# Two layer norms around a gated ConvFFN on one core: statistics from running sums, and an up-projection of rows that are not yet normalised

## What is computed

```python
x1 = layer_norm(ALPHA * x + mix @ w_out, ln1_w, ln1_b)
u, fconv_new = causal_dwconv(x1 @ w_up + b_up, fconv_prev, ffn_conv_w, ffn_conv_b)   # width 3
ff = (jax.nn.gelu(u[..., :D_FF]) * u[..., D_FF:]) @ w_down + b_down                  # D_FF = 2688
y = layer_norm(ALPHA * x1 + ff, ln2_w, ln2_b)
```

## Time and profile before

| | us |
|---|---|
| median of 3 runs | 1031.28 |
| lowest, highest | 1025.5, 1032.95 |
| profiled execution, whole | 1037.76 |
| profiled execution, span first to last instruction | 1036.1 |
| PE busy in it | 917.0 |
| DVE busy | 517.5 |
| ACT busy | 374.2 |
| POOL busy | 99.3 |

### The profile page before, as it was taken

One profiled execution on the slowest core, in us unless ns is written; L12 is line 12 of the kernel. 1 busy time (PEld: TensorE's weight loads), 2 busy tenths in 40 slices (PEclk: granted clock), 3 DMA queues, 4 the chain that ended last, 5 costly groups with the idle time before them and its releaser, 6 DMA issues.

```text
span 1036.1 us, 19860 instructions
## 1 busy us (share of the span) xinstructions
PE 917.0 (89%) x7903; PEld 821.8 (79%) x7903; DVE 517.5 (50%) x1116; ACT 374.2 (36%) x742; POOL 99.3 (10%) x164
## 2 busy tenths in 40 slices
PE   5999988998898667888869959999999999999993
PEld 5888877787776553655559839999999999999992
DVE  4522345522335566566752265766776677332325
ACT  4322344644421010345651155434433443222115
POOL 1012213343341002000000000000000000000000
PEclk9989999899896555569989969999999999999997
DMA  8247777676462001400022202222222222222212
GB/s 292 70 145 256 229 264 235 207 223 180 127 233 89 6 1 42 175 1 1 2 87 82 82 1 75 89 82 85 100 82 82 95 90 72 89 90 76 86 33 87
DMA packets 53152, 112.46 MB, mean 109 GB/s; under 512 B 6954, under 2 KB 30283, under 8 KB 52611
## 3 DMA queue, kind: packets, MB, share of 16 engines
q1 hardware_dynamic: 45648, 91.68, 25.9%
q0 software_dynamic: 6528, 17.83, 5.4%
q10 hardware_dynamic: 882, 1.67, 0.5%
HBM read 105.54 MB, written 12.40 MB: 114 GB/s over the span
## 4 chain that ended last, share of the span: by engine, by line
PE 80%; DVE 9%; ACT 4%; issue 3%; DMA 3%; ACTq 0%; POOLq 0%; POOL 0%; SPq 0%; DVEq 0%
PE q L1669 30%; PE q L1667 27%; PE q L2114 3%; DMA arena<-in_pool 2%; PE q L2142 2%; PE q L2132 2%; PE q L1731 1%; PE q L2175 1%; PE q L2176 1%; PE q L2002 1%; PE q L2056 1%; PE q L1719 1%; PE q L1785 1%; ACT whi L956 1%; PE q L1965 1%
## 5 line engine op out<-in xcount | busy, mean ns | idle before, releaser
L469 DVE TENSOR_TENSOR wring_r<-wring,whi_r 128x1024 fp32r<-128x1024 f32 (+1 forms) x101 | 120.5, 1194 | 341.8 <-ACT whi_r L466 341.7
L466 ACT ACTIVATE whi_r<-wring 128x1024 fp32r<-128x1024 f32 (+1 forms) x101 | 104.2, 1033 | 327.8 <-PE q L1669 316.9
L1669 PE MATMUL q<-xt_r,whi_r 128*128 128x288 f32 x552 | 166.9, 302 | 0.0
L1667 PE MATMUL q<-xt_r,whi_r 128*128 128x256 f32 x552 | 157.5, 285 | 0.0
L1667 PE MATMUL q<-arena_r,whi_r 128*128 128x256 f32 x440 | 137.6, 313 | 19.6 <-DVE xt_r L469 11.5
L1669 PE MATMUL q<-arena_r,whi_r 128*128 128x288 f32 x440 | 133.7, 304 | 0.0
L1669 PE MATMUL q<-arena_r,wring_r 128*128 128x288 f32 x440 | 133.0, 302 | 0.0
L1667 PE MATMUL q<-arena_r,wring_r 128*128 128x256 f32 x440 | 125.9, 286 | 0.0
L1667 PE MATMUL q<-mixt_r,whi_r 128*128 128x256 f32 x400 | 113.2, 283 | 10.5 <-DVE xt_r L469 10.5
L1669 PE MATMUL q<-mixt_r,whi_r 128*128 128x288 f32 x400 | 119.4, 298 | 0.0
L1667 PEld LDWEIGHTS q<-arena_r,whi_r 128*128 128x128 f32 x440 | 86.2, 196 | 27.4 <-issue 19.7
(11 more groups left out here) (406 smaller groups left out, 1584.1 us busy)
## 6 DMA issues: line engine op xcount, KB each, us to landing
wring<-in_w_up SPq DMA_DIRECT2D x42, 512.0 KB, 3.2
wring<-in_w_in SPq DMA_DIRECT2D x27, 512.0 KB, 5.1
arena<-in_pool SPq DMA_DIRECT2D x64, 192.0 KB, 3.1
arena<-in_pool POOLq DMA_DIRECT2D x64, 192.0 KB, 3.9
wring<-in_w_down SPq DMA_DIRECT2D x24, 448.0 KB, 3.1
arena<-in_pool SPq DMA_DIRECT2D x64, 64.0 KB, 2.1
arena<-in_pool POOLq DMA_DIRECT2D x64, 64.0 KB, 2.4
wring<-in_w_out SPq DMA_DIRECT2D x8, 512.0 KB, 7.3
```

The lines of the kernel that those rows point to most:

```text
L466: return eng.activation(out, src, ACT.Copy)
L469: return eng.tensor_tensor(out, src, hi.bitcast(F32), ALU.subtract)
L1667: pe.matmul(out[:, 0, 0:HALF], w, x[:, 0:HALF], start=(kk == 0 and n == 0), stop=(end and n == 2))
L1669: mm = pe.matmul(out[:, 1, 0:HALF + NS], w, x[:, HALF:NT], start=(kk == 0 and n == 0), stop=(end and n == 2))
```

## The change

- **Running sums.** In the out and down stages DVE keeps `total`, the sum of the rows so far, and `squares`, the sum of the squares that ACT makes. All rows are shifted by the mean of tile 0's rows times 8 (`shift`): PE makes it after four k steps of tile 1 (`first_mean`). The averages after each tile are gone.
- **Raw rows into the up stage.** The up tiles multiply the shifted, unnormalised rows times `ln1_w`, split as they come (`raw_high` on ACT, `raw_low` on DVE). Two more columns, `ln1_w` and `ln1_b` themselves, go along, so each tile's second matmul is 290 wide and its last two columns hold what the mean is to be multiplied by and the product with the bias.
- **Statistics per token in five columns.** `token_means` multiplies blocks of 128 tokens as the stationary operand with one column of `avg`, which gives mean and mean square of a token in a partition: five columns in all. DVE forms variance and reciprocal on those, spreads them over a diagonal, and PE's `spread` brings the factor of each token into every partition.
- **Mean and deviation at eviction.** In the up stage DVE's `scaled_rows` reads PSUM, subtracts and multiplies by `rstd`; ACT then writes `u` from SBUF, and takes over the convolution's first tap (`f_one`). The history copies go to POOL.
- **Down stage.** DVE rebuilds `ALPHA * x1 + b_down` from the raw rows (`residual`), then adds PSUM directly (`added`).

The core of the diff:

```diff
+        shift, total, squares, sq_m = (smem[:, NT * n:NT * n + NT] for n in range(4))
+        mean, rstd = dsc[:, 0:NT], dsc[:, NT:2 * NT]
...
+            for n in range(UP):
+                pool.wait_ge(f_u, n + 1)
+                pool.tensor_copy(fc[:, n, 0:2], uf[:, n % 4, 512:514])
+                pool.tensor_copy(fc[:, n, 2:18].rearrange("p (b t) -> p b t", b=NB),
+                                 by_sequence(uf, n, 6)[:, :, 4:6]).then_inc(f_last, 1)
...
+                if n == 0:
+                    root(0)
                 split_hi(act, I_UP + n + 2)
+                if n == 0:
+                    act.wait_ge(ln_pe, pe_stat(0, "mean"))
+                    act.activation(mean[:, 0:T].rearrange("p (c t) -> p c t", c=2), q4[2][:, :, 0:HALF], ACT.Copy)
+                    act.activation(mean[:, T:NT], q4[2][:, 1, HALF:HALF + NS], ACT.Copy)
+                    act.wait_ge(ln_pe, pe_stat(0, "spread"))
+                    act.activation(rstd[:, 0:T], bank[6], ACT.Copy)
+                    act.activation(rstd[:, T:NT], bank[7][:, 0:NS], ACT.Copy).then_inc(ln_act, 1)
                 if n >= 4:
                     act.wait_ge(f_conv, n - 3)
-                u = uf[:, n % 4, :]
+                    act.wait_ge(f_last, n - 3)
+                    act.wait_ge(f_done, (n - 4) // 2 + 1)
+                u, b, t = uf[:, n % 4, :], rowsum[:, n % 2:n % 2 + 1], scaled[n % 2]
                 us = by_sequence(uf, n, 6)
                 act.activation(us[:, :, 0:2], hf[:, n, :].rearrange("p (b t) -> p b t", b=NB), ACT.Copy)
-                act.activation(u[:, 2:514].rearrange("p (c t) -> p c t", c=2), q4[n % 2][:, :, 0:HALF],
-                               ACT.Identity, bias=vec("b_up", n))
-                act.activation(us[:, :, 2:6], q4[n % 2][:, 1, HALF:HALF + NS].rearrange("p (b t) -> p b t", b=NB),
-                               ACT.Identity, bias=vec("b_up", n)).then_inc(f_u, 1)
+                act.wait_ge(rw_u, n + 1)
+                act.activation(u[:, 2:514], t[:, 0:T], ACT.Identity, bias=b, scale=-1.0)
+                act.activation(us[:, :, 2:6], t[:, T:NT].rearrange("p (b t) -> p b t", b=NB), ACT.Identity,
+                               bias=b, scale=-1.0).then_inc(f_u, 1)
+                act.wait_ge(f_u, n + 1)
+                act.activation(tf[:, n % 4, 0:560], u[:, 0:560], ACT.Identity, bias=vec("fconv_b", n),
+                               scale=vec("fconv_w", n)).then_inc(f_one, 1)
...
+                    link(dve.tensor_tensor(t, raw_lo[:, m, 0:NT].bitcast(F32), raw_hi[:, m, 0:NT].bitcast(F32), ALU.add))
+                    link(dve.tensor_tensor(t, t, rstd, ALU.mult))
+                    link(dve.scalar_tensor_tensor(out=t, in0=mean, scalar=vec("ln1_w", m), in1=t, op0=ALU.mult,
+                                                  op1=ALU.subtract))
+                    link(dve.tensor_scalar(t, t, -ALPHA, var[:, m:m + 1], ALU.mult, ALU.add))
+                    if m >= 1:
+                        link(dve.tensor_tensor(t, t, shift, ALU.subtract))
...
+            def sums(base, m):
+                dve.wait_ge(ln_d, shifted_rows(base // KD, m))
+                link(dve.tensor_tensor(total, total, xt[:, m, :], ALU.add))
+            def sums_of_squares(base, m):
+                dve.wait_ge(ln_q, base + m + 1)
+                dve.tensor_tensor(squares, squares, sq_m, ALU.add).then_inc(ln_a, 1)
+                dve.wait_ge(ln_a, (KD - 1) * (base // KD) + m)
+            def raw_low(m):
+                dve.wait_ge(rw_hi, m + 1 if m == 0 else m + 2)
+                dve.scalar_tensor_tensor(out=raw_lo[:, m, 0:NT], in0=xt[:, m, :], scalar=vec("ln1_w", m),
+                                         in1=raw_hi[:, m, 0:NT].bitcast(F32), op0=ALU.mult,
+                                         op1=ALU.subtract).then_inc(rw_lo, 1)
...
+            def variance(n):
+                dve.wait_ge(ln_pe, pe_stat(n, "tokens"))
+                link(dve.tensor_copy(var[:, 8:13], bank[6][:, 0:5]))
+                link(dve.tensor_tensor(var[:, 8:13], var[:, 8:13], var[:, 8:13], ALU.mult))
+                dve.tensor_tensor(tok5[:, :], bank[7][:, 0:5], var[:, 8:13], ALU.subtract).then_inc(ln_dve, 1)
+            def inverse(n):
+                dve.wait_ge(ln_act, act_stat(n, "root"))
+                link(dve.reciprocal(tok5[:, :], tok5[:, :]))
+                dg = scaled[0]
+                dve.tensor_tensor(by_block(dg[:, 0:T]), ident.unsqueeze(1).broadcast_to([128, 4, 128]),
+                                  bc(tok5[:, 0:4], 128), ALU.mult)
+                dve.tensor_tensor(dg[:, T:NT], ident[:, 128 - NS:128], tok5[:, 4:5].broadcast_to([128, NS]),
+                                  ALU.mult).then_inc(ln_dve, 1)
...
+            def scaled_rows(n):
+                p, t = q4[n % 2], scaled[n % 2]
+                dve.wait_ge(w_used, I_UP + n + 1)
...
+                c1 = p[:, 1, HALF + NS:HALF + NS + 1]
+                dve.tensor_scalar(rowsum[:, n % 2:n % 2 + 1], p[:, 1, HALF + NS + 1:HALF + NS + 2], vec("b_up", n), None,
+                                  ALU.add)
+                dve.scalar_tensor_tensor(out=t[:, 0:T].rearrange("p (c t) -> p c t", c=2),
+                                         in0=mean[:, 0:T].rearrange("p (c t) -> p c t", c=2), scalar=c1,
+                                         in1=p[:, :, 0:HALF], op0=ALU.mult, op1=ALU.subtract)
+                link(dve.scalar_tensor_tensor(out=t[:, T:NT], in0=mean[:, T:NT], scalar=c1,
+                                              in1=p[:, 1, HALF:HALF + NS], op0=ALU.mult, op1=ALU.subtract))
+                dve.tensor_tensor(t, t, rstd, ALU.mult).then_inc(rw_u, 1)
             for n in range(UP):
+                if n == 0:
+                    variance(0)
+                    inverse(0)
                 split_lo(dve, I_UP + n + 2)
-                dve.wait_ge(f_u, n + 1)
+                scaled_rows(n)
+                dve.wait_ge(f_one, n + 1)
                 u, t = uf[:, n % 4, :], tf[:, n % 4, 0:560]
-                link(dve.tensor_scalar(t, u[:, 0:560], vec("fconv_w", n), vec("fconv_b", n), ALU.mult, ALU.add))
                 link(dve.scalar_tensor_tensor(out=t, in0=u[:, 1:561], scalar=vec("fconv_w", UP + n),
                                               in1=t, op0=ALU.mult, op1=ALU.add))
-                dve.tensor_copy(fc[:, n, 0:2], u[:, 512:514])
-                dve.tensor_copy(fc[:, n, 2:18].rearrange("p (b t) -> p b t", b=NB), by_sequence(uf, n, 6)[:, :, 4:6])
                 dve.scalar_tensor_tensor(out=t, in0=u[:, 2:562], scalar=vec("fconv_w", 2 * UP + n),
                                          in1=t, op0=ALU.mult, op1=ALU.add).then_inc(f_conv, 1)
...
+            for m in range(KD):
+                if m == 1:
+                    first_shifted(KD)
+                    link(dve.tensor_copy(total, xt[:, 0, :]))
+                residual(KD, m)
+                for c in range(DOWN_PARTS):
+                    i = I_DOWN + DOWN_PARTS * m + c
+                    if i + 2 < len(ITEMS):
+                        split_lo(dve, i + 2)
+                added(KD, m)
+                if 1 <= m < KD - 1:
+                    sums(KD, m)
+                    sums_of_squares(KD, m)
+            def centred(m):
+                dve.tensor_tensor(xt[:, m, 0:T].rearrange("p (c t) -> p c t", c=2),
+                                  xt[:, m, 0:T].rearrange("p (c t) -> p c t", c=2), q4[2][:, :, 0:HALF], ALU.subtract)
+                link(dve.tensor_tensor(xt[:, m, T:NT], xt[:, m, T:NT], q4[2][:, 1, HALF:HALF + NS], ALU.subtract))
+            dve.wait_ge(ln_pe, pe_stat(1, "mean"))
+            centred(0)
+            variance(1)
+            centred(1)
+            inverse(1)
+            for m in range(2, KD):
+                centred(m)
+            dve.wait_ge(ln_pe, pe_stat(1, "spread"))
+            for m in range(KD):
+                dve.tensor_tensor(xt[:, m, 0:T], xt[:, m, 0:T], bank[6], ALU.mult)
+                dve.tensor_tensor(xt[:, m, T:NT], xt[:, m, T:NT], bank[7][:, 0:NS], ALU.mult).then_inc(ln_u, 1)
...
+            def token_means(src, out, first=True, last=True):
+                for j, t in enumerate((0, 128, 256, 384, NT - 128)):
+                    mm = pe.matmul(out[:, j:j + 1], src[:, t:t + 128], avg[:, 0:1], start=(first and j == 0), stop=last,
+                                   skip_group_check=True)
+                return mm
...
+            def means():
+                pe.wait_ge(ln_a, KD - 1)
+                token_means(total, bank[6])
+                average(total, q4[2]).then_inc(ln_pe, 1)
+                token_means(squares, bank[7]).then_inc(ln_pe, 1)
+            def spread(n):
+                pe.wait_ge(ln_dve, 2 * n + 2)
+                pe.matmul(bank[6], ones, scaled[0][:, 0:T], start=True, stop=True)
+                pe.matmul(bank[7][:, 0:NS], ones, scaled[0][:, T:NT], start=True, stop=True).then_inc(ln_pe, 1)
...
             pe.wait_ge(np_mx, QT)
-            norm_pe(0, out_tile)
```

(22 more changed lines are left out.)

281 lines of the change are left out of this document (155 added, 126 removed).

## The result

| | before | after |
|---|---|---|
| median, us | 1032.12 (4 runs) | 1054.86 (4 runs) |
| lowest, highest of after | | 1053.58, 1059.41 |
| ratio, 95% interval | | 1.0242 (1.021 to 1.0275) |
| profiled span | 1036.1 | 1051.9 |
| from out tile 0's end to the last instruction | 491.3 | 512.8 |

The changed kernel is 22.7 us slower. The prediction was 1047 us, slower by over 1% with a chance of 0.65, and a range of 1030 to 1062. Sign and mechanism hold; the change was foreseen as 15.5 us and came out 7 us larger.

A forecast was written before the change was run, and what follows sets the result against it. It took the up stage, PE-bound before, to become bound by a DVE-ACT chain. The down stage's end 21.5 us late, less 6 in the second norm, gave +15.5 on the median of 1031.3: 1047 us, range 1030 to 1062.

The forecast's parts named there:

- rows of up tile 0: Up stage's start: tile 0, carrying the token statistics, has its rows leave 15.9 us after the start.
- a pair: Up stage: two successive up tiles, even and odd, take 14.58 us where PE needs 12.08.
- PE's wait in down tile 0: Down stage: PE stands 7.4 us before part 2 because DVE's `split_lo` comes late; the clock falls, costing 1.9 us.
- second norm: After the down stage: 22.2 us, with 0.8 for the colder clock 23; 6 us less than before.
- Out stage, and that the first norm's wait goes: Out tiles take 5.99 us, one average 0.91; up tile 0 starts without waiting, 31.7 us earlier.
- The chain: Up stage: DVE and ACT wait for each other in turn, links 4.79 us a tile; up 48.4 us longer.
- The PSUM scalar: Up stage's DVE scaling: a scalar read from PSUM costs 0.06 us; free or double moves the total about -7 or +8.
- The step from span to median: Final sum: the +15.5 us found on the profiled span was added to the median of 1031.3 us, giving 1047.
- the cheaper chain: Rival, up stage: PSUM scalars free, ACT at its PSUM price; a pair 14.03, whole 1036 us; chance 0.20.
- the estimate of 5.4 us: Up stage: by the skill's rule two new PSUM reads cost 0.06 us more each, over 42 tiles; not charged.
- POOL: Rival, up stage: POOL's 84 history copies block DVE, 0.34 us a tile, whole 1061 us; chance 0.12.
- The PE-bound stage: Rival: PE still sets the up stage's pace, up 258.3 us, whole 998 us; chance 0.12.

The follow-up runs named there:

- no_mul: The changed kernel with the multiplication by `rstd` left out of the up stage's `scaled_rows`; 1025.40 us, 0.9937 of before.
- tap_back: The changed kernel with the convolution's first tap back on DVE, as before the change; 1032.99 us, 0.9999 of before.
- lag: The changed kernel with DVE doing the taps of tile n - 1 behind the scaling of tile n, ACT's order unchanged; 1020.26 us, 0.9899 of before.
- lag_act: The changed kernel with DVE's taps one tile later and ACT's GELU and gate high part one tile later, behind the weight split; 1005.67 us, 0.9740 of before.
- short: The changed kernel with the third pass (low weights by high rows) left out of the up tiles; 1053.50 us, 1.0204 of before.
- wide: The changed kernel with token products 64 columns wide instead of one, only one of the 64 read; 1053.33 us (one run).
- down_first: The changed kernel with DVE's weight splits of the third and fourth down part ahead of `mean * rstd` and `residual`; 1050.15 us, 1.0201 of before.
- pool_later: The changed kernel with POOL's history copies waiting for `f_one` (ACT's first tap) instead of `f_u`; 1053.64 us, 1.0225 of before.

## Why the prediction was right, and where it was short

Moments are counted from up tile 0's start (581.63 us in the profile after); the first row, the pair, the wait, the other down tiles and the second norm are lengths.

| step | predicted | measured |
|---|---|---|
| out tile 0's end to up tile 0 | 42.7 | 42.6 |
| rows of up tile 0 leave | 15.9 | 18.1 |
| a pair | 14.58 | 14.60 |
| PE is done with up tile 41 | 304.0 | 308.5 |
| DVE's last tap ends | 314.9 | 318.9 |
| PE's wait in down tile 0 | 7.4 | 6.6 |
| down tile 0 ends | 329.3 | 334.0 |
| the other down tiles | 111.8 | 112.0 |
| second norm | 23 | 24.2 |
| end | 464.1 | 470.2 |

- **Out stage, and that the first norm's wait goes: right.** Tiles 5.98 to 5.99 us apart, tile 1 6.90 with `first_mean`, no wait ahead of up tile 0.
- **The chain, right in each link.** From start to start: row sum 0.13 (0.13 foreseen), 512 columns from PSUM 0.66 (0.66), 32 columns 0.28 (0.27), times `rstd` 0.76 (0.76), `u` 0.63 and 0.33 (0.62 and 0.33), tap 0.89 (0.88); then 2.90 on the even tiles (2.91) and 2.06 on the odd ones (2.09). DVE stands 1.89 us before L1756 (1.8). PE's waits read 1.36 and 0.56 (1.6 and 1.0), since they count from the last result; from start to start a pair has 14.60 - 12.21 = 2.4 us more than PE needs. `no_mul`, `tap_back`, `lag` and `lag_act` show that it is the chain, and not DVE's load, that sets the stage, and `short` that it is not PE's.
- **The PSUM scalar** costs as one from SBUF, as I took it. The Trainium skill's rule in "VectorE: DVE Perf Modes" (the section on the TRN2 errata), an extra for a PSUM source, is not borne out: L1741 averages 0.741 us, which is the 0.68 of 512 columns and 0.06 for the scalar, with nothing left over for the source. Without a scalar the same is seen at 512 columns, first from PSUM, then all from SBUF (the changed kernel's groups):

```profile
L1659 DVE TENSOR_TENSOR xt<-xt,q 128x512 f32<-128x512 f32 x15 | 10.3, 685 | 10.9 <-PE q L1819 10.8
L1726 DVE TENSOR_TENSOR zt<-smem 128x512 f32<-128x512 f32 x21 | 14.4, 684 | 0.1
```

- **Mis-sized: rows of up tile 0, 2.2 us.** 1.5 is the clock that fell behind the token products, by the two kinds of kernel in which it did not (`wide`, and `tap_back`). I had foreseen a warm stage. Why it falls in eight of nine kernels with one-column products and not in the ninth stays open. The other 0.7 is mostly the products themselves: twenty took 2.45 us, not 1.8.
- **Mis-sized: the first GELU, 1.3 us.** Its table load was in no row that I used. Before, the same load (at 635.4 us) was followed by 2.14 us in which ACT stood; in the chain it stands between tap and weight split. That it delays the stage by all of its length is read from the trace, not tried:

```profile
607.05 1.28 ACT L1047 ACT_TABLE_LOAD   x1
608.35 0.67 ACT L1047 ACTIVATE smem<-smem 128x560 f32<-128x560 f32 x1
```

- The pairs' 0.02 us makes 0.4 over the stage. These three make 3.9 of the 4.0 by the last tap.
- **Down tile 0**: PE's wait was 0.8 shorter than foreseen, and the part behind it, at half clock for its first 5.4 us, took 7.75 us where I had 5.3 + 1.9. From the last tap to the tile's end it is 15.1 us against 14.4. `down_first` shows the reason as named, DVE's rebuilding ahead of the third `split_lo`.
- **Second norm, 1.2 us**: forty passes of token products took 5.8 us, not 3.6, the last ten at half clock. The sum's 0.8 for the colder clock covers part of it.
- **The step from span to median** added the sum to the median of before, right in form: from out tile 0's end the sum was 15.5 and measured 21.5. That miss of 6.0 us is the terms above: 4.0 by the last tap, 0.7 and 0.2 to the down stage's end, 1.2 behind it, less 0.1 ahead. Against the median it is 8.1 us (1054.9 and 1046.8), because before came out 0.8 us over the median that I added to, and the medians lie 1.2 us further apart than the profiles.
- **Slips in the sums.** The listed parts of DVE's work per out tile make 4.7 us, not 4.3, which still fits in 5.99. DVE's own links make 10.4 us a pair, not 10.1 (it was busy 10.2). `u` at 0.57 instead of 0.62 takes 2 us off the stage, not 4, so the cheaper chain was 14.13 a pair at the prices given. DVE instructions that read PSUM are three a tile, not the two that the estimate of 5.4 us counts. None of these enters the forecast.
- **The rivals.** The cheaper chain is out by the pair (14.60, not 14.0 to 14.1). POOL is out by `pool_later`. The PE-bound stage did not come, but it is what `lag_act` makes of the same work.

## What to carry to other kernels

When a change makes a tile go from one in-order engine to a second and back to the first, add up the links of that loop, weight splits and other standing work between them included, and compare the sum with the bottleneck's tile; busy shares (57% and 38% here) did not show it. If the loop is longer, let the returning half work one tile behind, on both engines, before moving any work: here that was worth 49 us with not one instruction less, while relieving the busier engine of a tap had cost 22. Behind such a stage, put what the next one waits for (the weight split) ahead of the catching up.

## What the runs showed of the hardware

- PE's clock went from 2.4 to 1.2 GHz while PE was busy without a gap, right behind twenty one-column fp32 passes (589.0 to 592.4 us), and in the second norm at 1032.75 us, between the first and the last of forty. Of nine kernels with such passes eight had the first fall (not `tap_back`) and all nine the second; in the two kernels with 64 columns the clock held until the passes were done, both times. The wide passes cost nearly the same: twenty in 2.55 us against 2.45.
- In `short`, where PE stands 3.37 us ahead of every second tile, its mean clock from 620 to 900 us was 0.87, and the kernel was no slower for it, since PE wasn't the bound.
- A copy of 16 columns on POOL that came 0.15 us behind a DVE instruction with two SBUF inputs took 0.72 us instead of 0.20, until DVE's was done; DVE's stayed at 0.81. A copy of two columns that came 0.03 us behind it took its usual 0.19. The Trainium skill says that of the two the one that starts first has the shared port for its whole instruction ("SBUF — State Buffer", "SBUF: two separate sides"). The trace agrees for DVE first and the second copy; the first one was not held.
